# First layer's input projections: the input turned without its norm, queries and keys first, latent rows after the scores

## The reference, cut to what matters

```
u = rmsnorm(h, g_attn)                 # h = x: (256, 1024)
c_q, c_kv, k_r, q_s, k_s, v_s = split(u @ w_in)   # 384, 256, 32, 512, 512, 512 columns
q  = rmsnorm(c_q,  g_cq)  @ w_uq       # 768 columns
kv = rmsnorm(c_kv, g_ckv) @ w_ukv      # 1024 columns
# latent (MLA) attention from q, kv, k_r with rotary positions
# stick-breaking attention from q_s, k_s, v_s:
z = (q_s . k_s) * 64**-0.5             # 8 heads of 64, strictly causal mask
log_a = log_sigmoid(z) + (sum of log_sigmoid(-z) over later keys)
o_s = exp(log_a) @ v_s
```

## Time and profile before

| | us |
|---|---|
| median of three runs (1482.47 to 1484.3) | 1483.52 |
| the profiled execution's own time | 1484.91 |
| its span, from the first to the last instruction | 1483.2 |
| PE busy | 1325.2 (89%) |
| DVE busy | 473.2 (32%) |
| ACT busy | 393.0 (26%) |
| POOL busy | 60.9 (4%) |

### The profile page before, as it was taken

The page is one execution under the profiler, slowest core; times in us unless marked ns, Lnnn a source line. Parts: engine busy times, 40 slices in busy tenths (PEclk is TensorE's granted clock), DMA queues, the critical chain, the costliest instruction groups (busy, mean ns, idle before and its releaser), DMA issues.

```text
span 1483.2 us, 16746 instructions
## 1 busy us (share of the span) xinstructions
PE 1325.2 (89%) x6977; PEld 750.1 (51%) x6977; DVE 473.2 (32%) x749; ACT 393.0 (26%) x626; POOL 60.9 (4%) x118
## 2 busy tenths in 40 slices
PE   6978799999999998888988888889887998799998
PEld 6867543334333333233333333333224897699986
DVE  4486421120101101111021111110113685677765
ACT  4657111111111101010010100010003664655553
POOL 4000100000000000000000000000010410000000
PEclk9989899999999999999999999999998997899999
DMA  9424399999999999999999999999999863355530
GB/s 336 149 92 185 110 415 415 417 418 418 416 416 417 418 418 415 417 418 418 416 417 418 418 418 415 418 418 418 416 415 355 205 210 105 114 171 188 182 114 29
DMA packets 121884, 480.82 MB, mean 324 GB/s; under 512 B 8464, under 2 KB 43435, under 8 KB 89040
## 3 DMA queue, kind: packets, MB, share of 16 engines
q1 hardware_dynamic: 119344, 474.78, 80.9%
q0 software_dynamic: 2464, 4.95, 1.5%
HBM read 478.38 MB, written 1.31 MB: 323 GB/s over the span
## 4 chain that ended last, share of the span: by engine, by line
PE 57%; DMA 30%; ACT 6%; DVE 5%; issue 2%; SPq 0%; DVEq 0%; ACTq 0%
DMA ring<-in_w_dn_dram 22%; PE ps L1772 21%; PE ps L2068 13%; PE ps L2107 8%; DMA arena<-in_w_dn_dram 7%; PE ps L2032 4%; PE ps L2123 2%; ACT arena L841 1%; PE ps L2040 1%; PE ps L2079 1%; DVE W L1107 1%; ACT W L692 1%; PE ps L2093 1%; PE ps L2087 1%; PE ps L2021 1%
## 5 line engine op out<-in xcount | busy, mean ns | idle before, releaser
L2068 PE MATMUL ps<-ring,arena 128*64 128x512 f32 x1472 | 330.4, 597 | 6.3 <-DMA ring<-in_w_gu_dram 6.3
L2107 PE MATMUL ps<-ring,arena 128*64 128x512 f32 x760 | 178.8, 600 | 36.4 <-DMA ring<-in_w_dn_dram 35.9
L2068 PEld LDWEIGHTS ps<-ring,arena 128*64 128x64 f32 x1472 | 102.0, 137 | 216.0 <-issue 191.0
L1772 PE MATMUL ps<-W,X 128*128 128x512 f32 (+2 forms) x804 | 184.8, 392 | 20.1 <-DVE W L1107 13.3
L1772 PE MATMUL ps<-X,W 128*128 128x256 f32 x1632 | 198.9, 285 | 4.0 <-DVE X L1716 2.0
L1772 PEld LDWEIGHTS ps<-X,W 128*128 128x128 f32 x1632 | 197.8, 193 | 5.2 <-issue 2.5
L1107 DVE TENSOR_TENSOR W<-ring,W 128x2048 fp32r<-128x2048 f32 (+3 forms) x67 | 151.8, 2266 | 99.3 <-ACT W L692 99.3
L1772 PEld LDWEIGHTS ps<-W,X 128*128 128x128 f32 x804 | 153.1, 196 | 50.1 <-DVE W L1107 14.8
L1386 DVE TENSOR_SCALAR arena<-ps 128x512 f32<-128x512 f32 x32 | 22.1, 692 | 487.2 <-PE ps L2068 487.2
L692 ACT ACTIVATE W<-ring 128x2048 fp32r<-128x2048 f32 (+3 forms) x67 | 126.0, 1881 | 106.1 <-PE ps L1772 104.0
L854 ACT ACTIVATE arena<-arena 128x512 f32<-128x512 f32 x32 | 20.1, 630 | 468.9 <-DVE arena L1386 468.9
(11 more groups left out here) (335 smaller groups left out, 942.2 us busy)
## 6 DMA issues: line engine op xcount, KB each, us to landing
ring<-in_w_gu_dram SPq DMA_DIRECT2D x184, 1024.0 KB, 20.1
ring<-in_w_dn_dram SPq DMA_DIRECT2D x95, 1024.0 KB, 23.3
arena<-in_w_gu_dram SPq DMA_DIRECT2D x72, 1024.0 KB, 20.1
arena<-in_w_dn_dram SPq DMA_DIRECT2D x33, 1024.0 KB, 22.8
ring<-in_w_up_dram SPq DMA_DIRECT2D x22, 1024.0 KB, 5.1
ring<-in_w_in_dram SPq DMA_DIRECT2D x16, 1024.0 KB, 13.6
ring<-in_w_down_dram SPq DMA_DIRECT2D x11, 1024.0 KB, 4.9
ring<-in_w_o_dram SPq DMA_DIRECT2D x4, 1024.0 KB, 5.1
```

What stands on the lines that cost most here:

```text
L1772: y = e.matmul(o, l, r, start=start and i == 0, stop=stop and i == 2)
L2068: y = e.matmul(ps[c * 64:c * 64 + 64, use[0], :], xs[:, k, c0:c0 + CAP], w[:, half * D + c * 512:half * D + (c + 1) * 512], start=False, s ...
L2107: y = e.matmul(ps[c * 64:c * 64 + 64, DB, :], a, w[:, kk % 2, c * 512:(c + 1) * 512], start=kk == 0, stop=kk == KD - 1)
```

## The change: what it does

1. PE turns `h`, the plain input, as soon as it has landed. The factor r = 1/rms is computed beside that and goes in later: into the latent rows when they leave PSUM (scale r0), into the values (scale r0), into the scores as rqs = r/8 per query row, and into the keys by a product with r spread over all partitions (`rsb1`, from a small product with the diagonal `dg1`).
2. The first weight piece is loaded and split in two halves, interleaved with the parts of the turned input.
3. The order of the pieces is now queries and keys (0 to 3), latent rows (4 to 6), values (7, 8). PE multiplies the latent rows after the scores. With the pieces all other work of the stage moves: on DVE the root, r0, rqs, dg1 and the rotary angles stand ahead of split 1; the copy of `rsb1` stands between splits 1 and 2; the latent rows' norm stands after split 8; `stick_sums(0)` stands behind it, split 9 and the key's rotary part. On ACT, splits 6 and 7 stand between Abs, Exp and Ln, and the latent rows' copy after Ln.

```
 # the order of loads and pieces
+        L_qk = [cload(w_in, 672 + 256 * j) for j in range(4)]
         L_a = [kload(w_in, k, n, 0, 672) for k, n in ((0, 3), (3, 3), (6, 2))]
-        L_qk = [cload(w_in, 672 + 256 * j) for j in range(4)]
-        SPL = (L_a + L_qk + L_v + ...
+        SPL = (L_qk + L_a + L_v + ...
 # SP
+                if n == 0:
+                    e.dma_start(dst[:, 0:4], src[:, 0:4]).then_inc(s_first, 16)
+                    e.dma_start(dst[:, 4:8], src[:, 4:8]).then_inc(s_land[i], 16)
+                    continue
 # ACT
+            def first_split(half):
+                k = slice(4 * half, 4 * half + 4)
+                e.wait_ge(*((s_first, 16) if half == 0 else (s_land[0], 16)))
+                e.activation(halved(0)[0][:, k], loads[0][0][:, k], ACT.Copy).then_inc((s_hi0, s_hi)[half], 1)
+            e.wait_ge(*BK.emptied(U_c3))
+            for half in range(2):
+                parts("attn", U_xT, xin[0], KD, lambda k: col("g_attn", k), (4 * half, 4 * half + 2))
+                first_split(half)
             (the two squares) ; root("attn", 0, 0, 2)
+            split(1)
+            (Sin, Sin) ; q_columns(0) ; split(2) ; q_columns(1) ; split(3) ; split(4) ; split(5)
             (Abs x2)
+            split(6)
             (Exp x2)
+            split(7)
             (Ln x2)
+            (latent rows out of PSUM, scale=r0) ; split(8) ; (4 squares) ; (R8 copy) ; root("c", 0, 0, 4)
             split(9)
 # DVE
+            columns_in(3, U_c3, 0)
+            for half in range(2):
+                parts("attn", U_xT, *xin, KD, lambda k: col("g_attn", k), (4 * half, 4 * half + 2))
+                first_split(half)
             (means, over_root)
-            for t in range(2):
-                x = e.tensor_scalar(u[:, t, :], h[:, t, :], rs[:, t:t + 1], None, ALU.mult)
+            e.tensor_copy(r0, rs[:, 0:2])
+            e.tensor_scalar(rqs, rs[:, 0:2], SBS, None, ALU.mult)
+            for t in range(2):
+                x = e.tensor_scalar(dg1[:, t, :], ident[:, :], rs[:, t:t + 1], None, ALU.mult)
+            e.wait_ge(s_pos, 32)
+            (the rotary angles)
+            split(1)
+            e.wait_ge(*BK.filled(U_rs))
+            e.tensor_copy(rsb1, whole(U_rs, T)).then_inc(taken[U_rs[0]], 1)
+            split(2)
+            split(3)
+            for j in range(2):
+                x = U_qk[2 + j]
+                e.wait_ge(*BK.filled(x))
+                e.tensor_tensor(ksT[:, 2 * j:2 * j + 2, :], in_two(x), bc(rsb1.unsqueeze(1), [P, 2, T]), ALU.mult)
+                split(4 + j)
             (staged vectors; scores out with scalar=rqs in place of SBS)
+            split(6) ; split(7) ; (latent rows out, times r0) ; split(8)
+            (means, over_root, the four products of the latent norm) ; split(9) ; (rotary part of the key)
             stick_sums(0)
-            split(9)
             parts("c", ...) ; split(10) ; stick_sums(1) ; split(11)
 # PE
+            for i in range(4):
+                turned(U_xT[i], h, 2 * i, 2)
+            (piece 0: m = 0 waits for s_lo0 at k = 0 and for the second half at k = 4; then m = 1)
+            two_columns(1, U_qk[1])
+            claim(U_rs)
+            e.wait_ge(*normed["attn", 0])
+            for t in range(2):
+                y = e.matmul(ps[:, U_rs[0], t * P:(t + 1) * P], bc(onec, [P, P]), dg1[:, t, :], start=True, stop=True)
+            y.then_inc(full[U_rs[0]], 1)
+            two_columns(2, U_qk[2])
+            two_columns(3, U_qk[3])
             (staged vectors, scores, bias product)
+            (latent rows: pieces 4, 5, 6)
             (values: pieces 7, 8)
```

More of the change, by code:

```diff
@@ L158, in build_program @@
         mx, rsum, onec = sm[:, 120:136], sm[:, 136:152], sm[:, 152:153]
-        rqs = sm[:, 153:155]
+        rqs, r0 = sm[:, 153:155], sm[:, 156:158]
         posm = sm[:, 160:224].rearrange("p (t e) -> p t e", t=2)
@@ L179, in build_program @@
         R8 = u[0:8, 1, 512:1024]
+        rsb1, dg1 = ar(5120, T), ar(5376, 2, P)
         PT, junk_a = ar(3072, 3072), ar(8192, 2, 512)
@@ L396, in build_program @@
         U_xT = takes(4)
-        U_a = [takes(2) for _ in range(2)]
-        U_qk = takes(4)
+        U_qk = takes(2)
+        U_rs = take()
+        U_qk += takes(2)
         U_c = takes(3)
@@ L401, in build_program @@
         U_rb = take()
+        U_a = [takes(2) for _ in range(2)]
         U_v = takes(2)
@@ L712, in _, with q_columns @@
             root("attn", 0, 0, 2)
[L713 to L717, removed]
-            for t in range(2):
[L719 to L722, removed]
-                e.wait_ge(*BK.filled(U_qk[i]))
[L724 to L739, removed]
+            def q_columns(i):
+                e.wait_ge(*BK.filled(U_qk[i]))
+                e.activation(qsT[:, 2 * i:2 * i + 2, :], in_two(U_qk[i]), ACT.Copy).then_inc(taken[U_qk[i][0]], 1)
+            split(1)
+            e.wait_ge(*angle["sin", 0])
+            e.activation(cs[:, 1], ang, ACT.Sin).then_inc(wave.sem, 1)
+            e.wait_ge(*angle["cos", 0])
+            e.activation(cs[:, 0], ak, ACT.Sin).then_inc(wave.sem, 1)
+            q_columns(0)
+            split(2)
+            q_columns(1)
+            split(3)
+            split(4)
+            split(5)
             zl = ((Z[:, 0:1024], L[:, 0:1024], U_z0), (Z[:, 1024:3072], L[:, 1024:3072], U_z1[0] + U_z1[1]))
@@ L755, in _ @@
                 e.activation(l_, l_, ACT.Ln, bias=1.0).then_inc(logs, 1)
+            for t in range(2):
+                e.wait_ge(*BK.filled(U_a[t][0]))
+                e.activation(prow[:, t, 0:384], whole(U_a[t][0], 384), ACT.Copy,
+                             scale=r0[:, t:t + 1]).then_inc(taken[U_a[t][0][0]], 1)
+            split(8)
+            for a, b_ in ((0, 384), (384, 640)):
+                for t in range(2):
+                    c = 2 * (a > 0) + t
+                    e.wait_ge(*BK.emptied(U_a[t][a > 0]))
+                    e.activation(u[:, t, a:b_], prow[:, t, a:b_], ACT.Square,
+                                 accum_out=ss[:, c:c + 1]).then_inc(squares.sem, 1)
+            e.wait_ge(*BK.filled(U_rb))
+            e.wait_ge(*squares["c", 3])
+            e.activation(R8, ps[0:8, U_rb[0], :], ACT.Copy).then_inc(taken[U_rb[0]], 1)
+            root("c", 0, 0, 4)
             split(9)
@@ L762, in _ @@
             for t in range(2):
[L763 to L766, removed]
+                e.activation(vs[:, t, :], whole(U_v[t]), ACT.Copy, scale=r0[:, t:t + 1]).then_inc(taken[U_v[t][0]], 1)
             e.wait_ge(sticks, 1)
@@ L1144, in _ @@
[L1144 to L1184, removed]
@@ new lines, in _ @@
+            for c in (C1, C2, C3):
+                e.wait_ge(*own.now())
+                step(e.scalar_tensor_tensor(out=ang, in0=ak, scalar=-c, in1=ang, op0=ALU.mult, op1=ALU.add))
+            e.wait_ge(*own.now())
+            e.tensor_scalar(ang, ang, 3.1415925, -3.1415925, ALU.min, ALU.max).then_inc(angle.sem, 1)
+            e.wait_ge(*angle["sin", 0])
+            step(e.tensor_scalar(ak, ang, -1.0, None, ALU.mult))
+            e.wait_ge(*own.now())
+            step(e.tensor_tensor(ak, ak, ang, ALU.max))
@@ new lines, in _ @@
+            e.wait_ge(*own.now())
+            e.tensor_scalar(ak, ak, -1.0, math.pi / 2, ALU.mult, ALU.add).then_inc(angle.sem, 1)
+            split(1)
+            e.wait_ge(*BK.filled(U_rs))
+            e.tensor_copy(rsb1, whole(U_rs, T)).then_inc(taken[U_rs[0]], 1)
+            split(2)
+            split(3)
+            e.wait_ge(*BK.emptied(U_rs))
+            for j in range(2):
+                x = U_qk[2 + j]
+                e.wait_ge(*BK.filled(x))
+                e.tensor_tensor(ksT[:, 2 * j:2 * j + 2, :], in_two(x), bc(rsb1.unsqueeze(1), [P, 2, T]),
+                                ALU.mult).then_inc(taken[x[0]], 1)
+                split(4 + j)
```

116 lines of the change are left out of this document (80 added, 36 removed).

## The result

| | before | after |
|---|---|---|
| median of 15 runs, us | 1483.24 (1479.31 to 1487.32) | 1488.37 (1486.01 to 1491.84) |
| ratio of the times, with its 95% interval | | 1.0031 (1.0022 to 1.0040) |
| span of the profiled execution | 1483.2 | 1485.4 |
| w_ukv product starts | 96.05 | 101.33 |
| first expert starts | 177.56 | 183.24 |

The difference of the medians is 5.1 us, the ratio makes 4.6 of it. The two profiled spans differ by 2.2 only; single executions of one kernel lie up to 5 us from their median, so single spans don't decide here. The start of a stage in the first 190 us is steadier, and I read those, but each is from one execution too, and PE's clock can move it by up to 2.8 us (see the experiments).

The account below looks back on a forecast made before the run. PE's start of the w_ukv product was taken to set the end, one for one: 7.8 us lost up to piece 3, 3.2 won after, w_ukv 100.7 after 96.05 (+4.65), hence 1488.2 us against the 1483.52 median; range 1482.5 to 1493.

Parts of the forecast that it names:

- The two waits: DVE's angles wait for positions ahead of split 1 (PE idles 3.6 us); rsb1 copy waits for PE behind piece 1 (2.8).
- the row of 1.02 us: A POOL issue at 7.45 beside DVE's norm product, now gone; the prediction took 0.6 us off the positions' landing for it.
- The clock terms: PE's passes run slower after idling: 2.1 us lost in piece 1, 1.7 behind the second idle time (bounds 0 and 2.3).
- the wait for bank 7: Latent rows wait for their fourth bank, freed by DVE's score copies at 54.3; first two latent pieces end at 64.0.
- The scale factors cost nothing: In products and copies, scalar and spread operand stand in instructions that were there, so the norm's factors were priced at nothing.
- The first half: From the start to piece 3's end, predicted to lose 7.8 us; from there to w_ukv, predicted to win 3.2.
- The halves at nothing: Loading the first weights in two halves was priced at nothing, or up to 1 us if the first half comes later.
- The first expert 4 to 5 us later: A predicted sign in the changed kernel: with w_ukv at 100 to 101, the first expert starts 4 to 5 us later.
- Rival B: Not slower: positions are there when DVE asks, deciding point a landing at 13.4 or sooner; 1481 to 1482.5 us, chance 0.12.
- Rival C: The shift is absorbed: the experts' stream sets the end by its own start; all ends at 1483.5 us, chance 0.08.
- A: Both waits bite and more is late: positions 1 to 2 us later, or slow latent rows; 1491.5 us, chance 0.2.
- D: Faster by more than 3 us: positions in time and the late chain less serial; 1477.5 us, chance 0.07.

Follow-up runs that it names:

- positions first: The changed kernel with the transfers of the positions and inverse frequencies issued first on POOL's list: 1486.29 us, ratio 1.0014 to the kernel before.
- angles later: The changed kernel with DVE's rotary angles and ACT's two sines moved behind split 3: 1482.85 us, ratio 0.9990 to the kernel before.
- both, first weights whole: The changed kernel with angles and sines behind split 3, spreading product ahead of piece 1, first weights loaded and split whole: 1482.64 us, ratio 0.9993.
- first weights whole: The changed kernel with the first weights loaded and split whole, behind all parts of the input: 1485.68 us, ratio 1.0010 to the kernel before.
- positions last: The changed kernel with positions and inverse frequencies issued last on POOL's first list, behind the router weights: 1492.79 us, ratio 1.0057.
- factor sooner: The changed kernel with PE's small product that spreads the norm's factor moved ahead of piece 1: 1481.76 us, ratio 0.9988 to the kernel before.

## Why the prediction was right, point by point

| step | predicted | measured |
|---|---|---|
| transposes of h start | 6.4 | 6.25 |
| piece 0 ends | 18.6 | 18.8 |
| positions in, angles done, split 1 done | 16.9, 19.8, 22.1 | 16.66, 19.9, 22.05 |
| piece 1 starts, ends | 22.15, 30.1 | 22.11, 30.7 |
| piece 2 starts | 33.5 | 33.85 |
| piece 3 ends | 47.0 | 47.1 |
| first two latent pieces end | 64.0 | 64.9 |
| w_ukv | 100.7 (+4.65) | 101.33 (+5.3) |
| time | 1488.2 | 1488.37 |

- The two waits are the mechanism, and each was shown by taking it away: 5.5 and 6.6 us alone, 9.9 together. They do not add, and the traces say why. The latent rows start 7.0, 7.5 and 10.1 us sooner than in the changed kernel (46.51, 46.10 and 43.41 for 53.55). The two single gains make 4.35 more than the joint one, and the two clock losses of the changed kernel are 2.7 + 1.55: each run alone was rid of both of them.
- The issues of POOL did come sooner with DVE's norm product gone (positions from 11.01, before 11.68), as taken from the row of 1.02 us. The rule of the Trainium skill ("GPSIMD Engine Reference", section "1. Specifications"), by which two SBUF inputs contend as well, is not borne out here: with DVE's half split at 10.08 to 11.30, POOL's issue at 10.50 took 0.52 as the others.
- The clock terms were off in both directions: 2.7 where I took 2.1 behind the first wait, 1.55 where I took 1.7 behind the second. The runs spread from 0 to 2.8 for idle times of 1.7 to 7.5 us, so the term holds as a range, hardly as a number. That the sum came within 0.6 us at w_ukv is in part luck: another execution of the same order could move one such term by more than that. That the time came within 0.2 us is luck too, since the forecast added +4.65 to a median of 1483.52, and the measured shift was +5.1 on 1483.24.
- The stretch from piece 3's end to the end of the first two latent pieces took 0.8 us more than summed, and it was not the wait for bank 7: DVE's copies had freed that bank at 54.05, sooner than the 54.3 of the sum, and PE ran on. The sum's 64.0, less 11.1 for 72 passes at full clock, wants the latent rows to start at 52.9. They started at 53.62, since PE had its last six score products and the bias product in front (51.54 to 53.62 in the chain), which the sum left out.
- "The scale factors cost nothing" was nearly so. DVE's score copies with a factor per row took 0.70 each where they took 0.65, off the chain; ACT's two latent copies took 1.03 where they took 0.85, and these are on it.
- The first half lost 7.9 us (7.8 in the sum). The second won 2.6, where the sum had 3.2.
- "The halves at nothing" was right for their load and their instructions: ACT took both halves, at 8.99 and 11.36, without a wait for a transfer. The sum counts the idle time and the clock behind it as they fall with halves, so the forecast does not suffer. What it did not see is that halves are themselves a choice with a price: whole weights made the changed kernel 2.7 us faster.
- "The first expert 4 to 5 us later" was 5.7, a sum of w_ukv's 5.3 and 0.4 behind it.
- Rival B had the price of the positions too high: with them first, the gain was 2.1 of the 5.7, since the angles stay in front. Its condition was wrong as well. A landing at 13.4 could not make split 1 ready as piece 0 ends, for DVE came to the angles only at 15.82 even with the positions there, and the prediction's own sum had it busy until 16.5. Rival C fell with the last column of the table. A and D did not come.

## What to carry to other kernels

When work is moved to make an engine start sooner, write down what now stands ahead of the next producer in each in-order list: here thirteen tiny instructions, and one copy that waits for PE, cost more than the norm that was taken away. A wait of 0.8 us in the profile can hold 3 us of work behind it, so read what is queued, not only how long the wait is. And price an idle time of PE with the clock behind it (0 to 2.8 us here), and ask whether it lies where another wait covers it.

## What the runs showed of the hardware

What an idle time of PE costs in clock is not a matter of its length alone. These are idle times in front of 48 or 96 passes of 256 columns, and what the passes took over full clock (5.86 and 11.72 us):

| kernel, piece | idle, us | over full clock, us |
|---|---|---|
| positions first, 1 | 1.74 | 1.64 |
| changed, 2 and 3 | 2.71 | 1.55 |
| angles later, 2 and 3 | 2.72 | 0.06 |
| changed, 1 | 3.36 | 2.72 |
| both, first weights whole, 0 | 5.05 | 2.76 |
| first weights whole, 0 and 1 | 5.23 | 2.05 |
| positions last, 1 | 7.50 | 2.67 |

From 3.4 us on, a longer idle time cost no more. In "factor sooner" 36 passes took 6.86 us, where "angles later" had 4.57, behind an idle time of only 0.65. Each row is one execution, and what sets the loss stays open.

In the first 20 us of an execution the clock column of a window can mislead. In "both, first weights whole" (us, PE, PEld, DVE, ACT and POOL busy, granted clock, DMA share, GB/s)

```profile
15.13:20.90 5.77, 5.76 (x27) 5.77 (x28) 3.15 (x8) 2.00 (x2) 1.64 (x3) 1.00 1.08 345
```

27 passes of 256 columns in 5.77 us are 0.214 each, which is 1.2 GHz, while the column says 1.00: the first clock record of this trace lies at 21.1 us. The other 21 of the piece's 48 passes took 2.85 us, near full clock. Ahead of the first record the time per pass is the better clock.
